# Second attention of a two-layer trunk: barriers taken out, tensor-engine work in another order

## What is computed

```python
proj = xn @ w_in[i]
ya = stick_breaking_attention(...)          # branch A, 8 heads
yb, v_b = rwkv7_time_mix(...)               # branch B, a recurrence in chunks of 64
yc = swa_sink_attention(...)                # branch C, 8 query heads, 2 key heads, window 128
ga, gb, gc = jnp.split(jax.nn.sigmoid(pg), N_BRANCH, axis=-1)
merged = ga * (ya @ w_proj_a[i]) + gb * (yb @ w_proj_b[i]) + gc * (yc @ w_proj_c[i])
h = h + merged @ w_out[i]
...
h = h + (swiglu(...) if i % 2 == 0 else moe_swiglu(...))
```

```python
p = jax.nn.softmax(jnp.concatenate([s_band, s_meta, sink], axis=-1), axis=-1)
o = einsum(p_band, vb) + einsum(p_meta, v_meta)
```

## Time and profile before

| what | value |
|---|---|
| median of 3 runs | 2113.72 us (2110.80, 2113.72, 2124.87) |
| the profiled execution's own time | 2110.74 us |
| span of that execution in the profile | 2108.9 us |
| PE, PEld, DVE, ACT busy | 98%, 85%, 70%, 58% of the span |
| mean granted clock of PE | 0.994 of full |

### The profile page before, as it was taken

The page is one execution under the profiler, slowest core; times in us unless marked ns, Lnnn a source line. Parts: engine busy times, 40 slices in busy tenths (PEclk is TensorE's granted clock), DMA queues, the critical chain, the costliest instruction groups (busy, mean ns, idle before and its releaser), DMA issues.

```text
span 2108.9 us, 35827 instructions
## 1 busy us (share of the span) xinstructions
PE 2058.0 (98%) x15134; PEld 1787.1 (85%) x15134; DVE 1485.4 (70%) x1357; ACT 1230.1 (58%) x1142; POOL 22.0 (1%) x24
## 2 busy tenths in 40 slices
PE   9999999999999999999999999999999999999998
PEld 7877789999999787788998888888888888888886
DVE  6633438566455682444758888898988989888896
ACT  5454445444333446345447777777777777777675
POOL 0000100000000000010000000000000000000000
PEclk9999999999999999999999999999999999999999
DMA  6333205444443232110647989899898989989895
GB/s 253 120 82 122 61 3 200 160 170 190 160 182 121 80 140 84 77 43 24 228 161 303 375 323 380 332 368 370 336 372 329 373 346 360 367 334 372 329 374 203
DMA packets 75069, 485.58 MB, mean 230 GB/s; under 512 B 13496, under 2 KB 14648, under 8 KB 17224
## 3 DMA queue, kind: packets, MB, share of 16 engines
q1 hardware_dynamic: 73816, 481.93, 59.1%
q10 hardware_dynamic: 1136, 1.92, 0.3%
HBM read 482.08 MB, written 1.74 MB: 229 GB/s over the span
## 4 chain that ended last, share of the span: by engine, by line
PE 91%; DVE 5%; ACT 3%; issue 1%; DVEq 0%; ACTq 0%
PE PS L547 24%; PE PS L549 23%; PE PS L548 23%; PE PS L954 6%; DVE area L1813 2%; PE PS L820 2%; PE PS L838 2%; PE PS L1229 1%; PE PS L1238 1%; PE PS L695 1%; DVE WL L1813 1%; PE PS L862 1%; ACT WH L1389 1%; PE PS L901 1%; PE PS L807 0%
## 5 line engine op out<-in xcount | busy, mean ns | idle before, releaser
L1813 DVE TENSOR_TENSOR WL<-ring,WH 128x2048 fp32r<-128x2048 f32 x410 | 934.5, 2290 | 218.0 <-ACT WH L1389 109.6
L1389 ACT ACTIVATE WH<-ring 128x2048 fp32r<-128x2048 f32 x336 | 643.1, 1916 | 157.4 <-PE PS L549 154.9
L547 PE MATMUL PS<-WH,XGH 128*128 128x512 f32 x896 | 353.5, 395 | 0.5 <-DVE XGL L1813 0.5
L549 PE MATMUL PS<-WL,XGH 128*128 128x512 f32 x896 | 349.7, 390 | 0.0
L548 PE MATMUL PS<-WH,XGL 128*128 128x512 f32 x896 | 349.1, 390 | 0.0
L549 PE MATMUL PS<-XL,WH 128*128 128x272 f32 (+1 forms) x704 | 202.5, 288 | 0.0
L1381 ACT ACTIVATE WH<-ring 128x2048 fp32r<-128x2048 f32 x74 | 141.0, 1910 | 99.1 <-PE PS L549 99.0
L549 PEld LDWEIGHTS PS<-WL,XGH 128*128 128x128 f32 x896 | 168.2, 188 | 35.7
L547 PEld LDWEIGHTS PS<-WH,XGH 128*128 128x128 f32 x896 | 168.3, 188 | 34.4 <-DVE XGL L1813 0.7
L548 PEld LDWEIGHTS PS<-WH,XGL 128*128 128x128 f32 x896 | 168.4, 188 | 33.6
L547 PE MATMUL PS<-WH,HTH 128*128 128x512 f32 x448 | 176.6, 394 | 0.6
(11 more groups left out here) (358 smaller groups left out, 3496.1 us busy)
## 6 DMA issues: line engine op xcount, KB each, us to landing
ring<-in_experts SPq DMA_DIRECT2D x336, 1024.0 KB, 6.6
ring<-in_weights SPq DMA_DIRECT2D x114, 1024.0 KB, 6.8
ring<-in_weights SPq DMA_DIRECT2D x4, 576.0 KB, 4.7
ring<-in_weights SPq DMA_DIRECT2D x4, 512.0 KB, 4.1
cst<-in_consts SPq DMA_DIRECT2D x1, 1731.0 KB, 8.8
area<-in_x ACTq DMA_DIRECT2D x2, 512.0 KB, 4.5
out<-area SPq DMA_DIRECT2D x4, 256.0 KB, 2.0
bias_line<-lin SPq DMA_DIRECT2D x1, 672.0 KB
```

The lines of the kernel that those rows point to most:

```text
L547: pe.matmul(o, lh, rh, start=first, stop=False, skip_group_check=True)
L549: return pe.matmul(o, lh, rl, start=False, stop=last, skip_group_check=True)
L1389: act.activation(WH[(BASE + j + 1) % 3][:, :], ring[b][:, 2048 * (j % 2):2048 * (j % 2) + 2048], ACT.Copy).then_inc(S("w_hi"), 1)
L1813: tt = lambda o, a_, b_, op: dve.tensor_tensor(o, a_, b_, op)
```

## The change

Five things change, in both layers.

1. The two barriers around the second attention are gone on all three engines.
2. `window_values` (the transposes of the values, now into bank 4) and `scores(0)` stand inside head 7 of branch A, ahead of that head's last products. ACT's copy of `yA` into `YH` moves behind unit 0's exponential, and DVE's last `pair_out(3)` between the two halves of unit 0.
3. Inside the loop PE's order is now scores of u+1, transposes of u, gate tile 4+u, values of u. Gate tile 3 stands ahead of the loop. ACT copies gate tile 4+u behind the copy of the transposes and ahead of the copy of `yC`.
4. Gate tile 7 is issued in three pieces: products 0 to 2 inside unit 3, 3 and 4 behind `products_b(0)`, 5 to 7 behind `turn_rows(0)`. `products_h(0)` moves into unit 4 in layer 0; in layer 1 it stands ahead of `products_b(0)`.
5. DVE no longer waits for the transposes of the last unit.

The diff, cut to its core:

```diff
-            return 6 + n % 2 if n < SB_GATES else 5 + n % 3
+            return 6 + n % 2 if n < SB_GATES else 5 + (n - 1) % 3
...
-                def early_gate(n):
+                def early_gate(n, first=0, last=KT):
...
-                    if n == 2:
-                        pe.wait_ge(S("eg_copied"), 8 * l + 1)
-                    if n >= SB_GATES + 3:
+                    if n in (2, 3):
+                        pe.wait_ge(S("eg_copied"), 8 * l + n - 1)
+                    if n == 4:
+                        pe.wait_ge(S("ya_copied"), at("ya_copied", l, 3))
+                    if n >= 5:
                         pe.wait_ge(S("eg_copied"), 8 * l + n - 2)
-                    for k in range(KT):
+                    for k in range(first, last):
...
-                end_stage(pe, "pe")
...
+                    fill(h + 1)
+                    if h == 7:
+                        window_values()
+                        pe.wait_ge(S("am_done"), at("am_done", l, 6))
+                        scores(0)
                     pe.wait_ge(S("at_done"), at("at_done", l, h))
...
+                early_gate(3)
                 for u in range(N_UNITS[l]):
                     meta_q = u == 4
-                    ahead, behind = unit_gates(l, u)
-                    for n in ahead:
-                        early_gate(n)
+                    if u + 1 < N_UNITS[l]:
+                        pe.wait_ge(S("c_m"), at("c_m", l, u))
+                        scores(u + 1)
 
                     pe.wait_ge(S("c_p"), at("c_p", l, u))
...
                     ins.then_inc(S("c_t"), 1)
-                    if u + 1 < N_UNITS[l]:
-                        scores(u + 1)
-                    for n in behind:
-                        early_gate(n)
+                    if u < 3:
+                        early_gate(4 + u)
+                    elif u == 3:
+                        early_gate(7, 0, 3)
+                    else:
+                        products_h(0)
                     pe.wait_ge(S("c_tc"), at("c_tc", l, u))
...
+                if l:
+                    products_h(0)
                 products_b(0)
-                products_h(0)
+                early_gate(7, 3, 5)
                 turn_rows(0)
+                early_gate(7, 5, KT)
                 level_product(0, 1)
...
-                end_stage(act, "act")
...
-                    for n_ in ahead:
-                        gated_early(n_)
+                    if u == 0:
+                        act.wait_ge(S("ya_copied"), at("ya_copied", l, 3))
+                        act.activation(YH[0][:, :, :], yA[:, :, :], ACT.Copy).then_inc(S("x_hi"), 1)
+                        gated_early(3)
                     act.wait_ge(S("c_t"), at("c_t", l, u))
...
-                    for n_ in behind:
-                        gated_early(n_)
+                    if u < 3:
+                        gated_early(4 + u)
                     act.wait_ge(S("c_y"), at("c_y", l, u))
...
                 copied_rows(0)
+                gated_early(7)
...
-                pair_out(3)
-                end_stage(dve, "dve")
...
+                    if u == 0:
+                        pair_out(3)
                     dve.wait_ge(S("c_e"), at("c_e", l, u))
...
-                    dve.wait_ge(S("c_t"), at("c_t", l, u))
+                    if u + 1 < N_UNITS[l]:
+                        dve.wait_ge(S("c_t"), at("c_t", l, u))
...
-                end_stage(dve, "dve")
```

More of the change, by code:

```diff
@@ L346, in pieces_done @@
             return N_PIECES * l + g + 1
[L348 to L352, removed]
         n_linked = {}
@@ L851, in _, with window_values, scores @@
                 window_bufs = [None]
+                def window_values():
+                    pe.wait_ge(S("ya_copied"), at("ya_copied", l, 2))
+                    for w, (t0, n) in enumerate(((0, 80), (META, P), (META + 64, P), (META + 128, P))):
+                        ins = pe.transpose(PS[0:n, 4, w * P:(w + 1) * P], vC[:, t0:t0 + n], C("ident"))
+                    ins.then_inc(S("c_vt"), 1)
+                def scores(u):
+                    meta_q = u == 4
+                    for g in range(2):
+                        r = 64 * g
+                        for jp in range(1 if meta_q else 2):
+                            if meta_q:
+                                lhs, o, m = qCm[r:r + 64, :, :].rearrange("p a b -> p (a b)"), 0, 64
+                            else:
+                                lhs = qCx[r:r + 64, u, 2 * jp:2 * jp + 2, :].rearrange("p a b -> p (a b)")
+                                o, m = (80 if u == 0 else 144) * jp, P
+                            keys = [(0, META)] if meta_q else [(0, 80)] if u == 0 else [(0, META), (META + 64 * (u - 1), P)]
+                            for t0, n in keys:
+                                ins = pe.matmul(PS[0:m, g, o:o + n], lhs, kC[r:r + 64, t0:t0 + n], start=True, stop=True)
+                                o += n
+                    ins.then_inc(S("c_z"), 1)
                 zscores(0)
@@ L905, in _ @@
-                scores(0)
-                for u in range(N_UNITS[l]):
-                    meta_q = u == 4
-                    ahead, behind = unit_gates(l, u)
-                    for n in ahead:
-                        early_gate(n)
[L912 to L921, removed]
-                    if u + 1 < N_UNITS[l]:
-                        scores(u + 1)
-                    for n in behind:
-                        early_gate(n)
[L926 to L933, removed]
-                                            pTC[0:META, :, :].rearrange("p a b -> p (a b)")[:, 64 * g:64 * g + 64], start=True, stop=True)
-                        elif u == 0:
-                            ins = pe.matmul(PS[64 * g:64 * g + 64, 4, 0:256], vW[0:80, 0, vcols],
-                                            pTC[0:80, 2 * g:2 * g + 2, :], start=True, stop=True)
-                        else:
-                            pe.matmul(PS[64 * g:64 * g + 64, 4, 0:256], vW[:, u, vcols],
-                                      pTC[:, 2 * g:2 * g + 2, :], start=True, stop=False, skip_group_check=True)
-                            ins = pe.matmul(PS[64 * g:64 * g + 64, 4, 0:256], vW[0:META, 0, vcols],
-                                            pTm[0:META, 2 * g:2 * g + 2, :], start=False, stop=True, skip_group_check=True)
-                    ins.then_inc(S("c_y"), 1)
@@ L1525, in _ @@
                 gated_early(2)
-                end_stage(act, "act")
                 act.wait_ge(S("c_vt"), at("c_vt", l, 0))
-                act.activation(vW[0:80, 0, :], PS[0:80, 6, 0:P], ACT.Copy)
-                act.activation(vW[:, 1:4, :], PS[:, 6, P:4 * P].rearrange("p (a b) -> p a b", b=P), ACT.Copy).then_inc(S("c_vtc"), 1)
-                act.activation(YH[0][:, :, :], yA[:, :, :], ACT.Copy).then_inc(S("x_hi"), 1)
+                act.activation(vW[0:80, 0, :], PS[0:80, 4, 0:P], ACT.Copy)
+                act.activation(vW[:, 1:4, :], PS[:, 4, P:4 * P].rearrange("p (a b) -> p a b", b=P), ACT.Copy).then_inc(S("c_vtc"), 1)
                 for u in range(N_UNITS[l]):
```

40 lines of the change are left out of this document (36 added, 4 removed).

## The result

The changed kernel took 2132.28 us, median of nine runs (2127.68 to 2135.54), against 2113.72 us before (nine runs, 2105.95 to 2124.87). The ratio is 1.0085, with a 95% interval of 1.0065 to 1.0105. It is slower by 18.6 us, where +1.0 us was forecast, and outside the forecast's range of 2108 to 2121 us.

The account below looks back on a forecast made before the run. PE was taken as the bound, 91% of the chain, so only its waits counted. Layer 0's +1.2 us and layer 1's -0.2 made +1.0: 2111.7 us for a run like the profiled one, median 2113.2, range 2108 to 2121.

Parts of the forecast that it names:

- The way into unit 0: Layer 0, ahead of unit 0's transposes: waits go, -1.77 us; unit 1's scores come earlier, +1.64; together -0.13 us.
- The wait that comes in inside the loop: Layer 0 units: exponential held behind gate tile and values; PE waits 1.65 us a unit, 3.0 ahead of unit 3; +0.18 and +1.23.
- The way into the recurrence: Layer 0, unit 4's transposes to first level product: barrier goes, gate tile 7's pieces fill DVE's chain; 6.97 against 7.01 us.
- Layer 1: Whole stretch in layer 1: -1.57 us at the head, +3.28 in the units, -1.9 at the tail; -0.2 us.
- The sum: Both layers together: +1.0 us, 0.05%, with stretches of 53.9 us in layer 0 and 50.5 us in layer 1.
- layer 1's old fall: Gate tile 3 in layer 1 took 5.32 us under a low clock; the 1.61 us lost was counted as gone.
- the rival that had it fall: New waits in both layers bring PE's clock down; one fall per layer makes +4.2 or +5.8 us, 2116 to 2118; chance 0.35.

Follow-up runs that it names:

- The outer edits alone: Changed kernel with unit loop order and gate tile 7 as before; barriers out and head as changed: 2111.31 us, ratio 0.9979 to the kernel before.
- filled kernel: Changed kernel with 3 or 6 idle products, to a bank nobody reads, in each of PE's new loop waits: 2118.29 us, ratio 1.0010 to the kernel before.
- the version with the exponentials first: Changed kernel with ACT's exponentials of unit u+1 directly behind the copy of unit u's transposes: 2104.17 us, ratio 0.9944 to the kernel before.
- the two with half of the waits filled: Changed kernel with idle products only ahead of units 1 and 2 (2120.72 us), or only ahead of units 3 and 4 (2122.50 us).
- the version with the exponentials behind the gate copy: Changed kernel with unit u+1's exponentials on ACT between the copies of gate tile 4+u and yC: 2110.11 us, ratio 0.9980 to the kernel before.

## Why the prediction was wrong

Step by step, in the order in which the prediction has them.

- **The way into unit 0** was right. From gate tile 2 to unit 0's transposes it took 198.45 - 186.95 = 11.50 us; 195.71 - 183.94 - 0.13 = 11.64 was forecast. The outer edits alone gained 4.0 us.
- **The wait that comes in inside the loop** was right in its place, cause and size: 1.50, 1.25 and 2.91 us in layer 0, 1.50, 1.49 and 3.13 in layer 1, each ended by DVE with the exponential behind the `yC` copy. Taking the exponential out from behind it took all of them away.
- **The way into the recurrence** was right in that the pieces of gate tile 7 fill DVE's chain. It took 8.91 us, not 6.97: the granted clock was 0.52 in 240 to 242. In the filled kernel, at full clock, it took 237.77 - 230.38 = 7.39 us.
- **Layer 1**: the fall at gate tile 3 went, as forecast.
- **The sum** was right for a clock that stays up. The filled kernel is that case: 53.56 and 50.07 us, where 53.9 and 50.5 were forecast.
- **The step that failed is the clock**: the term in the sum that had it at full after layer 1's old fall was counted out, and the rival that had it fall, with a chance of 0.35 and a price of one fall of 1.6 us a layer, which made 2116 to 2118 us. It fell four times in the stretch of layer 0 and twice in that of layer 1, in both profiles of the kernel. That added 8.2 us in layer 0 and 4.3 us in layer 1 (61.72 - 53.56 and 54.40 - 50.07).

The price was too low for two reasons. First, I put one fall into each layer, at the longest wait. With the 1.5 us waits empty there are falls beside them too, and two of the four in layer 0 lasted about 7 us, where the fall of the earlier trace rows that I took the price of 1.61 us from lasted 3.6 (865.4 to 869.0). My argument against the rival was that the gate tile behind the 1.32 us of the earlier trace rows ran at full speed. One such wait between busy stretches was no evidence for three or four in a row, and the row showed nothing of falls without a wait beside them. Second, the new order puts the gate tile into the chain. In the kernel before a slow gate tile lies beside the exponentials. In the changed one the `yC` copy, and the next exponential behind it, wait for it. So the slow products lengthen the very step that ends in the next wait: 12.60 and 9.10 us in place of 10.39 and 6.39.

The Trainium skill says of the clock (page "TensorE: Matmul & The Clock Gate", section "HAM oscillation — how this bites in real kernels") that pauses between bursts of products bring it to half. The filled kernel agrees: the same order with no pause in it kept the clock at 1.00 in both stretches. But the version with the exponentials first had a fall at 211.0 us with 0.2 us of idle time in the whole stretch, and the changed kernel one at 216.2 us ahead of its wait. So a pause directly ahead is not needed for a fall. These falls began under the scores of 128x16 or as they ended; the filled kernel has the same scores without a fall, and no run separates what brings one on.

The rest of the 23.1 us of span lies where nothing was changed: 3.0 us ahead of gate tile 2, 2.6 in the first recurrence, and falls in the router stage. By (1 - clock) the router stage lost 8.5 us in the changed kernel in both profiles, 8.5 in the filled one too, 1.7 in the kernel before, and 0 to 8.5 in the other versions. Since the filled kernel had it as well, it is no part of the 14.6 us between that and the changed kernel; whether it has a part in the 3.0 us that are left is open, and so is why it differs.

## What to carry over

When an edit adds waits to PE, price the low clock as well as the wait, for each wait and not once, and add what the products lose under it if they lie in the chain. The low stretches here lasted 3.5 to 7.0 us, and in the two layers they made 12.5 us of stretch. To find out which of the two a loss is, fill the waits with products that nobody reads and that are no longer than the waits: the order stays and the clock changes. And before moving work between two steps on one engine, read what the other engines have queued behind the step that is now later; here one move on ACT turned 18 us lost into 11 us gained.

## What the runs showed of the hardware

- Nine waits of 1.25 to 1.6 us stood empty on PE in layer 0's unit loop, over four profiles of the new order (the changed kernel twice, and the two with half of the waits filled). Each had a fall to 1.2 GHz beside it, which began between 0.6 us ahead of the wait and 0.4 us behind its end. Single waits of 1.32 us (layer 0) and 1.54 us (layer 1) in the kernel before had none. In layer 1 the first wait of 1.50 us had none in either profile of the changed kernel.
- Filling waits of 1.5 to 3 us with 3 to 6 products of 128x256 kept the clock at 1.00 over 53.6 and 50.1 us, and gave back 14.6 us of a run.
- The clock can fall with PE busy. In the version with the exponentials first it was 0.96 over layer 0's stretch, whose PE was idle for 0.2 us in it. In the version with the exponentials behind the gate copy it fell 10.3 us behind the last wait, and in the changed kernel at 216.2 us, 0.6 us ahead of the next wait and 9.7 behind the last.
- The kernel before itself spreads over 18 us (2107.2 to 2125.6 in 29 runs), and its granted clock goes with it (0.996 and 0.987 at the two ends). In its one profile 10.2 us are low clock.
